# A fused two-block layer: token-major projection first, convolution behind it, norm weight folded into the first norm

## What is computed

```python
u = rms_norm(x, norm_mix_g)              # x * rsqrt(mean(x*x) + 1e-6) * g, 512 x 1024
p = u @ w_in                             # w_in is 1024 x 8208
qa, ka, va, oa, i, f, qb, kb, vb, ga, gb = split(p)   # qa, ka: 512 each; va: 1024; i, f: 8 each; ...
qk = silu(causal_conv([qa, ka], conv_w)) # four taps along the tokens
v  = va                                  # no convolution
logf = log_sigmoid(f)                    # cumulative sums and maxima along the tokens follow
...                                      # mLSTM heads (8), stick-breaking heads (8), w_out, MLP, second block
```

## Time and profile before

| what | us |
|---|---|
| median of 3 runs | 1357.5 |
| profiled execution | 1358.28 |
| its span, first to last instruction | 1356.6 |
| PE busy with matmuls | 1314.5 (97% of the span) |
| DVE busy | 763.5 (56%) |
| ACT busy | 679.5 (50%) |
| POOL busy | 201.7 (15%) |
| first matmul of a product (L633) starts | 20.07 |
| last matmul of the four `va` slabs ends (the heads begin) | 121.1 |

### The profile page before, as it was taken

How to read it: one execution, slowest core, us unless ns; L and a number is a source line. 1 busy time by engine, 2 the same in 40 slices (tenths; PEclk the granted TensorE clock), 3 DMA queues, 4 the chain that set the end, 5 groups by cost and what they waited for, 6 DMA issues and landing times.

```text
span 1356.6 us, 17827 instructions
## 1 busy us (share of the span) xinstructions
PE 1314.5 (97%) x7149; PEld 1098.8 (81%) x7149; DVE 763.5 (56%) x1217; ACT 679.5 (50%) x1053; POOL 201.7 (15%) x265
## 2 busy tenths in 40 slices
PE   6999999999999999999999999899999999999998
PEld 4887777787788887878878787788899998989876
DVE  4753444434544544595775858721266767776563
ACT  5244555347666424454635546445245667665232
POOL 1101332261000000000000000003612333331000
PEclk9999999999999999999999999999999999999999
DMA  8657443394435334134070420372612222222311
GB/s 172 103 121 115 73 85 70 88 205 113 62 63 62 81 106 159 59 114 135 1 236 12 154 95 1 93 221 78 139 38 72 71 71 71 69 94 66 108 63 62
DMA packets 94817, 128.97 MB, mean 95 GB/s; under 512 B 5839, under 2 KB 70463, under 8 KB 94736
## 3 DMA queue, kind: packets, MB, share of 16 engines
q1 hardware_dynamic: 88528, 108.70, 31.9%
q0 software_dynamic: 6064, 18.83, 5.3%
q10 hardware_dynamic: 144, 0.31, 0.1%
HBM read 124.94 MB, written 2.88 MB: 94 GB/s over the span
## 4 chain that ended last, share of the span: by engine, by line
PE 86%; DVE 7%; ACT 3%; DMA 2%; issue 2%; SPq 0%; POOL 0%; DVEq 0%; ACTq 0%
PE ps_g L633 44%; PE ps_g L656 8%; PE ps_z L656 8%; PE ps_t L1277 6%; PE ps_z L1388 3%; PE ps_z L1425 2%; PE ps_z L1277 2%; PE ps_t L1460 2%; DVE w_lo L610 2%; DMA w_raw<-in_w_in 2%; PE ps_t L1155 1%; ACT w_hi L602 1%; PE ps_t L1193 1%; PE ps_z L1207 1%; PE ps_t L1310 1%
## 5 line engine op out<-in xcount | busy, mean ns | idle before, releaser
L610 DVE TENSOR_TENSOR w_lo<-w_raw,w_hi 128x2048 fp32r<-128x2048 f32 (+1 forms) x84 | 193.5, 2304 | 233.0 <-ACT w_hi L602 233.0
L633 PE MATMUL ps_g<-act_hi,w_hi 128*128 128x512 f32 x784 | 310.3, 396 | 6.4 <-DVE act_lo L754 4.3
L633 PE MATMUL ps_g<-act_hi,w_lo 128*128 128x512 f32 x784 | 306.7, 391 | 0.0
L633 PE MATMUL ps_g<-act_lo,w_hi 128*128 128x512 f32 x784 | 306.5, 391 | 0.0
L602 ACT ACTIVATE w_hi<-w_raw 128x2048 fp32r<-128x2048 f32 (+1 forms) x84 | 159.2, 1895 | 113.3 <-PE ps_g L656 62.1
L633 PEld LDWEIGHTS ps_g<-act_hi,w_hi 128*128 128x128 f32 x784 | 148.0, 189 | 39.3 <-issue 5.0
L633 PEld LDWEIGHTS ps_g<-act_hi,w_lo 128*128 128x128 f32 x784 | 148.0, 189 | 31.5
L633 PEld LDWEIGHTS ps_g<-act_lo,w_hi 128*128 128x128 f32 x784 | 148.1, 189 | 29.7
L633 PE MATMUL ps_g<-w_hi,act_hi 128*128 128x256 f32 x320 | 93.4, 292 | 0.0
L633 PE MATMUL ps_g<-w_lo,act_hi 128*128 128x256 f32 x320 | 90.3, 282 | 0.0
L633 PE MATMUL ps_g<-w_hi,act_lo 128*128 128x256 f32 x320 | 90.2, 282 | 0.0
(11 more groups left out here) (349 smaller groups left out, 2602.0 us busy)
## 6 DMA issues: line engine op xcount, KB each, us to landing
w_raw<-in_w_in SPq DMA_DIRECT2D x32, 1024.0 KB, 9.2
w_raw<-in_nsa_w_in SPq DMA_DIRECT2D x22, 1024.0 KB, 5.2
w_raw<-in_w_up SPq DMA_DIRECT2D x16, 1024.0 KB, 5.6
down_raw<-in_w_down SPq DMA_DIRECT2D x16, 1024.0 KB, 5.2
tile_t<-bias_rev_dram POOLq DMA_DIRECT2D x32, 256.0 KB, 3.1
bc<-stat_rows_dram POOLq DMA_DIRECT2D x24, 256.0 KB, 10.2
w_raw<-in_w_out SPq DMA_DIRECT2D x4, 1024.0 KB, 5.0
w_raw<-in_nsa_w_out SPq DMA_DIRECT2D x4, 1024.0 KB, 5.0
```

The source lines that it names most:

```text
L610: nc.vector.tensor_tensor(slab_view(w_lo[b], n), slab_view(raw(n), n), slab_view(w_hi[b], n).bitcast(F32), ALU.subtract).then_inc(lo_done, 1)
L633: mm = nc.tensor.matmul(o, stationary, moving, start=(k == 0 and j == 0), stop=(k == KT - 1 and j == 2))
```

## The change

The slabs are used in another order: the first pair of `va` half slabs, the `if` slab, the four `conv` slabs, the second pair of `va` half slabs, and then `qb` as before. The first `va` half slab is loaded in two pieces between the first and the second token block of x. Its low part is made by DVE for the first piece and by POOL for the second. The norm's weight comes in as one row, PE spreads it over the partitions by a product with ones into `ps_g`, and DVE multiplies x, the inverse root and that weight in one instruction. PE no longer transposes everything first: for each token block it transposes, ACT and DVE make the high and low parts of four features at a time, and the matmuls of a block are issued with the transposes of the next block among them. The transposed vectors, the bias rows and their copies move behind the first pair of `va` slabs, ahead of the `if` slab. The gate arithmetic of DVE and ACT moves to the first `conv` slab (`N_QA`), ACT's second Exp to the second one. A Sqrt on one element loads that table ahead of the first block.

```diff
+        N_VA = add_wide("va", W, VA, 1)
+        N_IF = add("if", W, IF, 1, w=P)
         N_QA = add("conv", W, QA, 4)
-        N_IF = add("if", W, IF, 1, w=P)
-        N_VA = add_wide("va", W, VA, 2)
+        N_VA2 = add_wide("va", W, VA, 1, s0=1)
...
@@ block.sync
-            for b in range(TB):
+            sp.dma_start(x_sb[:, 0, :], x_rows[:, 0, :]).then_inc(x_in[0], 16)
+            first_rows = W[0:HALF_K * P, VA:VA + WIDE].rearrange("(k p) n -> p k n", p=P)
+            sp.dma_start(first_pieces(w_raw[0], 0), first_rows[:, 0:2, :]).then_inc(first_w_in, 16)
+            sp.dma_start(first_pieces(w_raw[0], 1), first_rows[:, 2:4, :]).then_inc(raw_landed[0], 16)
+            for b in range(1, TB):
                 sp.dma_start(x_sb[:, b, :], x_rows[:, b, :]).then_inc(x_in[b], 16)
-            for name, (r0, k) in VEC_PARTS[:SYNC_VECS]:
-                sp.dma_start(vec_rows[r0:r0 + k, :], a[name]).then_inc(vec_in, 16)
-            for n in range(N_MLP):
-                if n == 1:
-                    sp.wait_ge(raw_landed[0], 16)
+            for n in range(1, N_MLP):
+                if n == 2:
+                    sp.wait_ge(first_w_lo, 1)
+                    for name, (r0, k) in VEC_PARTS[:SYNC_VECS]:
+                        sp.dma_start(vec_rows[r0:r0 + k, :], a[name]).then_inc(vec_in, 16)
                 load_slab(n)
@@ block.tensor
+            def first_turns(b):
+                pe.wait_ge(xn_ready, b + 1)
+                for j in range(2):
+                    if b >= 2:
+                        pe.wait_ge(first_lo, 2 * (b - 2) + j + 1)
+                    for k in range(4):
+                        mm = nc.tensor.transpose(first_bank(b, j)[:, k * P:(k + 1) * P],
+                                                 xn[b][:, (4 * j + k) * P:(4 * j + k + 1) * P], ident)
+                    mm.then_inc(first_t, 1)
+            ...
+            first_turns(0)
+            pe.wait_ge(first_w_lo, 1)
+            for b in range(TB):
+                t, m = tile_of[N_VA] + b, slice(b * P, (b + 1) * P)
+                if b == 2:
+                    pe.wait_ge(xn_ready, TB)
+                pe.wait_ge(first_hi, 2 * b + 1)
+                for k in range(HALF_K):
+                    if k == 2:
+                        pe.wait_ge(lo_done, 1)
+                    nc.tensor.matmul(bank(t), act_hi[:, k, m], wh[:, k, :], start=(k == 0), stop=False)
+                    nc.tensor.matmul(bank(t), act_hi[:, k, m], wl[:, k, :], start=False, stop=False)
+                    if k == 0:
+                        pe.wait_ge(first_lo, 2 * b + 1)
+                    mm = nc.tensor.matmul(bank(t), act_lo[:, k, m], wh[:, k, :], start=False, stop=False)
+                    if k == 2 and b < TB - 1:
+                        first_turns(b + 1)
+            mm.then_inc(half_done, 1)
+            for b in range(TB):
+                pe.wait_ge(first_lo, 2 * b + 2)
+                mm_half(pe, N_VA + 1, b)
+            turn_vectors()
+            bias_rows()
+            mm_slab(pe, N_IF)
             for n in range(N_QA, N_QA + 4):
-                mm_slab(pe, n, activation_ready=features_ready(pe, n, 0) if n == N_QA else None)
+                mm_slab(pe, n)
+            mm_slab(pe, N_VA2)
@@ block.scalar
+            order.link(nc.scalar.activation(ssq[0:1, 0, 0:1], ones_row[0:1, 0:1], ACT.Sqrt))
+            ...
+            first_squares(0)
+            first_root(0)
+            act.wait_ge(first_w_in, 16)
+            nc.scalar.copy(first_pieces(w_hi[0], 0), first_pieces(w_raw[0], 0)).then_inc(first_w_hi, 1)
+            act.wait_ge(raw_landed[0], 16)
+            nc.scalar.copy(first_pieces(w_hi[0], 1), first_pieces(w_raw[0], 1)).then_inc(hi_done, 1)
+            first_high(0, 0)
+            first_squares(1)
+            ...
             act.wait_ge(vec_ready, 1)
-            for n in range(N_QA, N_QB):
-                if n != N_IF:
+            for n in range(N_VA, N_QB):
+                if n not in (N_VA, N_IF):
                     split_hi(act, n + 1)
-                if n == N_VA:
+                if n == N_QA:
                     wait_tile_free(act, tile_of[N_IF])
                     order.link(nc.scalar.activation(rows[0][:], rows[2][:], ACT.Abs))
...
-                    if n == N_IF - 1 and i == 1:
+                    if n == N_IF - 1 and i == TB - 1:
                         split_hi(act, N_IF + 1)
...
-                if n == N_VA + 2:
+                if n == N_QA + 1:
                     act.wait_ge(gate_dve, 1)
                     nc.scalar.activation(rows[1][:], rows[1][:], ACT.Exp, scale=-1.0).then_inc(gate_act, 1)
@@ block.vector
+                nc.vector.scalar_tensor_tensor(xn[b][:], x_sb[:, b, :], r, ps_g[:].rearrange("p a n -> p (a n)"),
+                                               ALU.mult, ALU.mult).then_inc(xn_ready, 1)
+            ...
             dve.wait_ge(vec_t, 1)
...
+            dve.wait_ge(oh_mm, 1)
+            nc.vector.tensor_copy(bias_rev_sb[:], ps_t[0:HN, 512:1152]).then_inc(oh_cp, 1)
+            nc.vector.tensor_copy(bias_fwd_sb[:], ps_t[:, 1152:1152 + 8 * HN]
+                                  .rearrange("p (c h) -> p c h", h=HN)).then_inc(oh_cp, 1)
-            for n in range(N_QA, N_QB):
+            for n in range(N_VA + 1, N_QB):
                 split_lo(dve, n + 1)
                 for i in range(0 if k_half(n) == 0 else tiles_of(n)):
                     dve_evacuate(dve, order, n, i)
                 if n == N_QA:
-                    dve.wait_ge(oh_mm, 1)
-                    ...
-                if n == N_VA:
                     wait_tile_free(dve, tile_of[N_IF])
                     dve.wait_ge(gate_act, 1)
                     ...
@@ block.gpsimd
+            pool.wait_ge(hi_done, 1)
+            nc.gpsimd.tensor_tensor(first_pieces(w_lo[0], 1), first_pieces(w_raw[0], 1),
+                                    first_pieces(w_hi[0], 1).bitcast(F32), ALU.subtract).then_inc(lo_done, 1)
```

More of the change, by code:

```diff
@@ L409, in add, with add_wide @@
             return first
-        def add_wide(kind, mat, col0, n, row0=0):
+        def add_wide(kind, mat, col0, n, row0=0, s0=0):
             first = len(slabs)
-            for i in range(n):
+            for i in range(s0, s0 + n):
                 for half in range(2):
@@ L717, in wait @@
                 if k >= 2:
-                    pe.wait_ge(norm_lo, 6 * which + k - 1)
+                    pe.wait_ge(norm_lo, 6 * (which - 1) + k - 1)
                 elif k == 1:
@@ L1090, in turn_vectors @@
                 pe.wait_ge(vec_in_pool, 16 * (len(VEC_PARTS) - SYNC_VECS + 2))
-                nc.tensor.transpose(ps_g[:, 0, 0:V_ROWS], vec_rows[:], ident[0:V_ROWS, 0:V_ROWS])\
+                nc.tensor.transpose(ps_z[:, 1024:1024 + V_ROWS], vec_rows[:], ident[0:V_ROWS, 0:V_ROWS])\
                     .then_inc(vec_t, 1)
-                pe.wait_ge(vec_ready, 1)
-            feature_tiles(pe, N_QA, lambda b: xn[b], lambda b: pe.wait_ge(xn_ready, b + 1), turn_vectors)
-            for n in range(N_QA, N_QA + 4):
-                mm_slab(pe, n, activation_ready=features_ready(pe, n, 0) if n == N_QA else None)
-                if n == N_QA:
-                    pe.wait_ge(nsa_in, 32)
-                    nc.tensor.matmul(ps_t[0:HN, 512:1024], table[:], onehot[:, OH_REV:OH_REV + 512],
-                                     start=True, stop=True)
-                    nc.tensor.matmul(ps_t[0:HN, 1024:1152], table[:],
-                                     onehot[:, OH_REV + 512:OH_REV + 640], start=True, stop=True)
-                    for c in range(8):
-                        mm = nc.tensor.matmul(ps_t[:, 1152 + HN * c:1152 + HN * (c + 1)],
-                                              onehot[:, c * P:(c + 1) * P], table[:], start=True,
-                                              stop=True)
-                    mm.then_inc(oh_mm, 1)
@@ L1111, in _, with bias_rows @@
-            mm_slab(pe, N_IF)
-            mm_slab(pe, N_VA)
-            mm_slab(pe, N_VA + 1)
-            mm_slab(pe, N_VA + 2)
+            def bias_rows():
+                pe.wait_ge(nsa_in, 32)
+                nc.tensor.matmul(ps_t[0:HN, 512:1024], table[:], onehot[:, OH_REV:OH_REV + 512],
+                                 start=True, stop=True)
+                nc.tensor.matmul(ps_t[0:HN, 1024:1152], table[:],
+                                 onehot[:, OH_REV + 512:OH_REV + 640], start=True, stop=True)
+                for c in range(8):
+                    mm = nc.tensor.matmul(ps_t[:, 1152 + HN * c:1152 + HN * (c + 1)],
+                                          onehot[:, c * P:(c + 1) * P], table[:], start=True,
+                                          stop=True)
+                mm.then_inc(oh_mm, 1)
@@ new lines, in _ @@
+            pe.wait_ge(ones_set, 1)
+            for c in range(2):
+                mm = nc.tensor.matmul(ps_g[:, c, :], ones_row[0:1, 0:P], gain_row[:, c * 512:(c + 1) * 512],
+                                      start=True, stop=True)
```

(7 more changed lines are left out.)

119 lines of the change are left out of this document (93 added, 26 removed).

## The result

The changed kernel takes 1374.35 us (median of 4 runs, 1372.61 to 1374.68), the kernel before 1358.15 in runs of the same kind (1356.93 to 1359.63). The ratio on record is 1.0114, with a 95% interval from 1.0101 to 1.0127 (the two medians alone give 1.0119): slower, as forecast, but outside the range of 1355 to 1370. The profiled execution has a span of 1372.7 us and not 1362.7: 16.1 more than before, where the working gave 6.1. So 10.0 us are to be found.

A forecast was written before the change was run, and what follows sets the result against it. TensorE, busy 97% of the span, was taken as the bound, waiting on DVE and ACT between `conv` slabs. 5.3 gained against 2.3, 1.6, 8.4 and 0.9 lost made 6.1 later: median 1363.6, range 1355 to 1370.

The forecast's parts named there:

- The start: From x's landing to the bias rows: first matmul at 12.4, bias rows done at 43.7, 5.3 us gained.
- the turn to the `if` slab: Behind the bias rows: DVE's copies and narrow low split start the `if` slab at 46.05 instead of 43.7, 2.3 lost.
- The three waits for L850: TensorE waits for banks that DVE frees among the `conv` slabs: 3.3, 3.0 and 2.1, together 8.4 us.
- the half clock behind 47.34: Stall ahead of the `if` slab lets TensorE's clock fall: 1.6 us lost behind 46.05.
- POOL's half: POOL's part of the first slab's low split: taken as 2.7 us, between 1.15 and 3.97; either end costs nothing.
- The load of the second `conv` slab: Issued at 46.05 into the `if` slab's buffer: 13.9 us, landing at 60.0, low split ended at 64.2.
- In nobody's way: The `if` tile's evacuation waits for the bias write until 54, 8.4 behind 45.1, and delays nothing.
- The second Exp: On ACT among the `conv` slabs, behind Silu: Exp with its table load takes 1.9 us, a switch 1.3.
- Slow clock after the stalls is covered: Among the `conv` slabs: the chain through DVE sets each start, not TensorE, so low clock there adds nothing.
- (a): Rival, chance 0.18: TensorE stays the bound among `conv` slabs; point at 118.8, 2.3 earlier, 1355.3; 1353 without late `if` split.
- (b): Rival, chance 0.17: second `conv` slab's load takes 8.7 like the fourth; end 124.1, 3.0 later, 1360.5.
- (c): Rival, chance 0.15: first slab's pieces land late, 1371, or the four blocks run at 1.2 GHz, 1372.

The follow-up runs named there:

- bias_apart: Changed kernel with the bias rows in buffers of their own, so the `if` evacuation doesn't wait for their write: 1371.85 us, ratio 1.0102.
- writes_late: bias_apart with both bias writes issued by POOL only when the second `conv` slab has landed: 1366.24 us, ratio 1.0056.
- rev_late: bias_apart with only the 640 KB `bias_rev` write held until the second `conv` slab has landed: 1367.94 us, ratio 1.0076.
- exp_later: Changed kernel with ACT's second Exp moved from the second `conv` slab to the second pair of `va` slabs: 1370.94 us, ratio 1.0090.
- before_late_once: Kernel before, shifted by loading the first block of x once more and waiting for it ahead of everything: 1361.54 us, ratio 1.0026.
- gates_spread: Changed kernel with bias_apart and exp_later edits, `if` splits ahead of the vectors' transpose, DVE's gate operations spread behind three `conv` slabs' tiles: 1356.76 us, ratio 0.9994.

## Why the prediction was right and where it was wrong

Right was the direction, and most of its mechanism: the start gained, the turn to the `if` slab lost 2.30 us (forecast 2.3), the gates lay between the tiles and TensorE waited for banks among the `conv` slabs. The three waits for L850, forecast at 3.3, 3.0 and 2.1, were not as told: there were two, 6.30 for the `if` tile's rows and 2.91 for a `conv` tile. In place of the third TensorE was busy, since behind the 2.91 it ran at half clock. In bias_apart there are three, 6.87, 1.01 and 1.60, all for a `conv` tile. Right were also the small terms: DVE's scaling 1.28 (1.24), and the half clock behind 47.34 (2.3 us on 48 matmuls, forecast 1.6), which cost nothing, as the late slab set the next start.

Three terms were mis-sized, one step failed (with a clause on the clock that went with it) and one effect was missing. Along the path:

- **The start, +1.3.** The second piece of the first slab landed at 12.0 and not at 10.8, so the first matmul began at 13.69 (12.4), the third tile at 24.09 (22.8), and the bias rows ended at 45.05 (43.7). POOL's half took 2.37 us; I had taken 2.7 between 1.15 and 3.97, and it cost nothing. Of the 1.3 a part is this execution's: the other seven with the same start have 0.6 to 2.4. The Trainium skill's figure in "GPSIMD Engine Reference", section "3.1 Elementwise", from which the estimate was 2.3, agrees with this row.
- **The load of the second `conv` slab, +4.4.** "It is this slab's own row and I take it" was right: 13.3 to 13.5 in every run of the new order without the large write beside it. But the row was taken from a place without that company, while the text itself had the bias write beginning 1 us ahead. 640 KB beside it cost 4.8 (writes_late, rev_late). The forecast had named this contention for its own range, but with 15 us as the upper end for the load. The low split of the slab ended at 69.84 and not at 64.2.
- **"In nobody's way": the step that failed, +2.4.** The term was put at nothing. The bias write was to end at 54, by its row of 8.4. It ended at 65.4 together with the slab (two writes stand behind that wait, and the second was never looked at), while TensorE needed the `if` tile's bank at 60.6. It waited until 67.03 and then needed 8.35 us for 24 matmuls that take 5.45 at full clock. VectorE had finished the first tile at 72.98 and waited 2.42 us for the second, which was evacuated 8.0 us later than forecast where the late load alone would have made it 5.6. At full clock the tile would have been there at 72.5 (an estimate: 67.03 + 5.45), before VectorE asked for it. So it took both, the bank held by the write and the low clock behind it. bias_apart takes the bank away and gives 2.6 back.
- **The second Exp, +1.3.** Its load of a table was counted, but not that the Silu after it takes the table away again: the heads' first Exp needs it once more, 1.28 at 137.87, with everything waiting. In the kernel before the Exp comes behind the last Silu, and the heads' Exp starts at 123.44 without a load; exp_later takes the load away. As to the price of a switch, Silu ended at 92.68, the load began at 92.70 and the Exp followed at 93.99: the drain of 1.38 us that the Trainium skill ("ScalarE: Activation LUTs", "What ACT_TABLE_LOAD costs") adds can't be seen in these rows.
- **"Slow clock after the stalls is covered"** failed at the first stall, as just told: 2.9 us of it, and VectorE waited 2.42. Behind the second stall it was covered by 0.04 us, in bias_apart and writes_late, where waits for VectorE follow, with more to spare; in exp_later it is the bound.
- **The clock behind the heads, +0.7.** Nothing was put down for it. 16.1 at the end against 15.4 at the heads is within what a mere shift does (before_late_once: 0.8 more, and 1.6 in between).

1.3, 4.4, 2.4, 1.3 and 0.7 make 10.1 of the 10.0 us. Each of the middle three was taken away by an experiment; the first is read from the trace alone, and the last only matched in size.

As to the rivals: (a), TensorE as the bound, is not what this change did, but it is what gates_spread does from 74.03 on. There the `va` slabs end at 118.4; (a) has 118.8 with a late `if` split and 2.3 less, 116.5, without one, as in that run, so that 1.9 are missing. (b), a load of 8.7, was seen in no run with these columns, whose best is 13.0 (before_late_once). (c), late pieces or a low clock through the four blocks, didn't come: the pieces landed at 8.4 and 12.0, and after nine product matmuls and eight transposes, from 18.6 on, the matmuls came at full pace. What stood on no list was the second write, which lands with the load and holds a bank.

## What to carry to other kernels

When a load is moved, ask what else is on the queues at its new time, and price it with that company; when a tile's evacuation waits for a write, look up every write behind the wait and the bank that is held meanwhile. When a buffer's release moves, follow the load that it triggers: one split that freed the buffer 14 us sooner gave back 12.5 of 15.4 us, more than any other single edit. When work must go between tiles of a chain that has no slack, cut it to the size of the idle gaps (2.5 us here), and let a function that needs another table run last before work that wants the same table.

## What the hardware showed that I had not expected

- The landing of a 1 MB load depends on which 256 columns it reads: 13.0 to 13.9 us for the second slab where no large write is beside it, 8.7 for the fourth in the kernel before; reading the fourth's columns in the second's place moved it by 4.9 us. Among the eight `qb` slabs of the kernel before, cut in the same way, it is again the second and the sixth that are slowest, 14.2 and 13.1, with the others at 7.6 to 12.2.
- A write of 640 KB issued 0.9 us ahead of such a load delays it by 4.8 us, while its own landing stays at 8.2 to 8.4 (8.4 in the kernel before). A 64 KB write in 64-byte pieces lands in 3.4 us with the slow load beside it but no large write ahead, in 8.5 behind the large write in the kernel before, and in 18.0 with both.
- The same idle time of 2.4 us in the same code leaves TensorE's granted clock at 1.00 or brings it down to 0.59 in the next 4 us, by when it comes. The low clock behind a stall costs 1.6 to 2.9 us in the changed kernel and exp_later. So a gain of 1 to 3 us at one point of this kernel can be gone 200 us later, and only the marks along the trace tell it from a gain that was never there.
